# Four in-place split buffers for the weight slabs of a two-layer transformer block in fp32

## What is computed

```python
z = rmsnorm(x, ln1) @ w_in
merged = (sigmoid(ga) * (o_a @ w_pa) + sigmoid(gb) * (o_b @ w_pb)
          + sigmoid(gc) * (o_c @ w_pc))
x = x + merged @ w_o
u = causal_dwconv(rmsnorm(x, ln2) @ w_up, conv_w, conv_b)
a, b = split(u, 2)
x = rmsnorm(x + (silu(a) * b) @ w_down, ln_f)
# second layer
y = concatenate([y_conv, y_rwkv]) @ w_out          # both from rms_norm(x, g0) @ w_in_2
x = x + rms_norm(y, g1)
y = memory_cross_attention(rms_norm(x, g2), mem_n, wq, wkv, wo)
x = x + rms_norm(y, g3)
y = swiglu(rms_norm(x, g4), w_gu, w_down_2)
x = x + rms_norm(y, g5)
```

## Time and profile before

| what | us |
|---|---|
| median of three executions | 914.25 |
| the profiled execution | 913.55 |
| its span in the profile | 911.7 |
| PE busy in it | 858.5 (94%) |
| DVE busy | 567.5 (62%) |
| ACT busy | 440.0 (48%) |
| POOL busy | 20.8 (2%) |
| transfers | 145.86 MB, 160 GB/s in the mean |

### The profile page before, as it was taken

One profiled execution on the slowest core, in us unless ns is written; L12 is line 12 of the kernel. 1 busy time (PEld: TensorE's weight loads), 2 busy tenths in 40 slices (PEclk: granted clock), 3 DMA queues, 4 the chain that ended last, 5 costly groups with the idle time before them and its releaser, 6 DMA issues.

```text
span 911.7 us, 18606 instructions
## 1 busy us (share of the span) xinstructions
PE 858.5 (94%) x7952; PEld 797.7 (87%) x7952; DVE 567.5 (62%) x671; ACT 440.0 (48%) x558; POOL 20.8 (2%) x31
## 2 busy tenths in 40 slices
PE   4999999998999999998988989999899799999997
PEld 4899999987999998888986889888897799999885
DVE  4475467476777776647599886566554655555444
ACT  4555755445555556436472401445544544444333
POOL 1110000000000002000000000000000000000000
PEclk9999999999999999999999999999999799999999
DMA  9853433556455555455433121144524355555541
GB/s 346 287 183 115 173 139 139 186 208 220 160 176 180 184 179 191 179 185 202 168 125 110 48 96 50 48 155 160 171 95 141 112 185 184 184 184 184 185 139 46
DMA packets 22253, 145.86 MB, mean 160 GB/s; under 512 B 2618, under 2 KB 2810, under 8 KB 6064
## 3 DMA queue, kind: packets, MB, share of 16 engines
q1 hardware_dynamic: 19008, 134.23, 42.2%
q0 software_dynamic: 2896, 10.13, 3.4%
q10 hardware_dynamic: 288, 0.59, 0.2%
HBM read 143.87 MB, written 1.07 MB: 159 GB/s over the span
## 4 chain that ended last, share of the span: by engine, by line
PE 79%; DVE 12%; ACT 4%; issue 3%; DMA 1%; DVEq 0%; ACTq 0%
PE ps L1629 23%; PE ps L1631 22%; PE ps L1630 22%; DVE w_lo L935 4%; ACT w_hi L470 2%; PE ps L2025 2%; PE ps L1973 1%; PE ps L1657 1%; DVE cacc L1293 1%; DMA norm_gain<-in_rows_vec 1%; DVE xn L1525 1%; PE ps L2190 1%; PE ps L2206 1%; DVE xn L989 1%; DVE x L1531 1%
## 5 line engine op out<-in xcount | busy, mean ns | idle before, releaser
L935 DVE TENSOR_TENSOR w_lo<-raw,w_hi 128x2048 fp32r<-128x2048 f32 x124 | 284.8, 2297 | 189.2 <-ACT w_hi L470 189.2
L1629 PE MATMUL ps<-hT_hi,w_hi 128*128 128x256 f32 x1240 | 356.2, 287 | 13.2 <-DVE hT_lo L996 7.1
L1630 PE MATMUL ps<-hT_lo,w_hi 128*128 128x256 f32 x1240 | 352.9, 285 | 0.0
L1631 PE MATMUL ps<-hT_hi,w_lo 128*128 128x256 f32 x1240 | 352.9, 285 | 0.0
L470 ACT ACTIVATE w_hi<-raw 128x2048 fp32r<-128x2048 f32 x125 | 239.1, 1912 | 174.6 <-PE ps L1631 174.1
L1629 PEld LDWEIGHTS ps<-hT_hi,w_hi 128*128 128x128 f32 x1240 | 240.2, 194 | 19.0 <-issue 16.1
L1630 PEld LDWEIGHTS ps<-hT_lo,w_hi 128*128 128x128 f32 x1240 | 240.1, 194 | 0.1
L1631 PEld LDWEIGHTS ps<-hT_hi,w_lo 128*128 128x128 f32 x1240 | 240.1, 194 | 0.0
L1629 PE MATMUL ps<-w_hi,gT_hi 128*128 128x512 f32 x176 | 69.8, 397 | 0.6 <-DVE w_lo L935 0.6
L1631 PE MATMUL ps<-w_hi,gT_lo 128*128 128x512 f32 x176 | 69.0, 392 | 0.0
L1630 PE MATMUL ps<-w_lo,gT_hi 128*128 128x512 f32 x176 | 68.4, 388 | 0.0
(11 more groups left out here) (286 smaller groups left out, 1043.2 us busy)
## 6 DMA issues: line engine op xcount, KB each, us to landing
raw<-in_weights SPq DMA_DIRECT2D x126, 1024.0 KB, 4.9
row_gain<-in_rows_vec POOLq DMA_DIRECT2D x4, 512.0 KB, 4.8
norm_gain<-in_rows_vec POOLq DMA_DIRECT2D x4, 512.0 KB, 4.7
bias<-bias_scratch POOLq DMA_DIRECT2D x1, 1536.0 KB, 9.5
x<-in_x SPq DMA_DIRECT2D x2, 512.0 KB, 5.2
xn<-in_mem POOLq DMA_DIRECT2D x2, 512.0 KB, 5.8
out<-x SPq DMA_DIRECT2D x4, 256.0 KB, 2.1
masks<-in_masks POOLq DMA_DIRECT2D x1, 768.0 KB, 12.4
```

The costliest lines, as they stand in the source:

```text
L935: V.tensor_tensor(w_lo[:, n % SPLIT, :], raw[:, n % RAW, :], w_hi[:, n % SPLIT, :].bitcast(F32), ALU.subtract).then_inc(sems["lo_ready"], 1)
L1629: mm(dst, left[0], right[0], start=first, stop=False)
L1630: mm(dst, left[0], right[1], start=False, stop=False)
L1631: return mm(dst, left[1], right[0], start=False, stop=last)
```

## The change

`w_lo` gets the memory of `raw`: it is laid over it with four buffers, so DVE overwrites each loaded slab by its low half. `w_hi` gets four buffers too; the total memory stays the same. A load into a buffer may then start only when PE has used the slab before in it, so SP waits for `slab_used` in place of `lo_ready`, and ACT's own wait for `slab_used` is gone. All `splits` and the splits in the loops reach one slab further (`AHEAD = 1`). At five places a call of `splits` is moved behind `fill_normed` or shortened by one slab, and `split_around` gives way to a whole split after the gating.

```diff
 RAW = 4
-SPLIT = 2
+AHEAD = 1
...
-        raw = sb("raw", [P, RAW, SLAB])
-        w_hi = sb("w_hi", [P, SPLIT, SLAB], F32R)
-        w_lo = sb("w_lo", [P, SPLIT, SLAB], F32R)
+        whole = ExitStack()
+        raw = sb("raw", [P, RAW, SLAB], F32, whole)
+        whole.close()
+        w_lo = sb("w_lo", [P, RAW, SLAB], F32R)
+        w_hi = sb("w_hi", [P, RAW, SLAB], F32R)
...
# SP
-                    sp.wait_ge(sems["lo_ready"], turn * RAW + (s + 1))
+                    sp.wait_ge(sems["slab_used"], turn * RAW + (s + 1))
...
# ACT, split and splits
-                if n >= SPLIT:
-                    act.wait_ge(sems["slab_used"], n - SPLIT + 1 + SLABS_PER_TURN * turn)
-                A(w_hi[:, n % SPLIT, :], raw[:, n % RAW, :], ACT.Copy).then_inc(sems["hi_ready"], 1)
+                A(w_hi[:, n % RAW, :], raw[:, n % RAW, :], ACT.Copy).then_inc(sems["hi_ready"], 1)
-                while next_slab[0] <= min(last, SLABS - 1):
+                while next_slab[0] <= min(last + AHEAD, SLABS - 1):
...
# ACT and DVE, the loops
-                    split(n + s + 2, turn)
+                    split(n + s + 2 + AHEAD, turn)
...
# DVE
-            split_around(gate_place(8)[0], lambda: gated(1, 0))
-            for q in range(1, 4):
+            for q in range(4):
                 gated(1, q)
-                if q == 2:
+                if q == 0:
                     outputs(3)
+            splits(gate_place(8)[0])
...
-            splits(FIRST_SLAB["up"])
+            splits(FIRST_SLAB["up"] - 1)
             add_acc("w_o")
             normed("ln2")
             fill_normed("ln2")
+            splits(FIRST_SLAB["up"])
...
             normed("g0")
+            fill_normed("g0")
             splits(FIRST_SLAB["in2"])
-            fill_normed("g0")
...
             normed("g2")
+            fill_normed("g2")
             splits(FIRST_SLAB["wq"])
-            fill_normed("g2")
...
-            splits(FIRST_SLAB["gu2"])
             add_normed("y3", 2)
             normed("g4")
             fill_normed("g4")
+            splits(FIRST_SLAB["gu2"])
```

More of the change, by code:

```diff
@@ L380, in _ @@
             for n in range((turns + 1) * RAW, SLABS):
-                sp.wait_ge(sems["lo_ready"], n - RAW + 1)
+                sp.wait_ge(sems["slab_used"], n - RAW + 1)
                 sp.dma_start(raw[:, n % RAW, :], weights[n]).then_inc(raw_in[n % RAW], 16)
@@ L670, in _ @@
                 up_pair(2, turn)
-            next_slab[0] = FIRST_SLAB["down"] + 2
+            next_slab[0] = FIRST_SLAB["down"] + 2 + AHEAD
             g_high(0, PAIRS - 1)
@@ L898, in gu_pair @@
                 n, u = FIRST_SLAB["gu2"] + 2 * p, FIRST_UNIT["gu2"] + 2 * p
-                split(n + 1, turn)
+                split(n + 1 + AHEAD, turn)
                 src = unit(u, turn)
@@ L906, in gu_pair @@
                     gu_high(p - 1, turn)
-                split(n + 2, turn)
+                split(n + 2 + AHEAD, turn)
             def gu_high(p, turn=0):
@@ L918, in _ @@
                 gu_pair(2, turn)
-            next_slab[0] = FIRST_SLAB["down2"] + 1
+            next_slab[0] = FIRST_SLAB["down2"] + 1 + AHEAD
             gu_high(PAIRS - 1)
@@ L934, in split @@
                 dve.wait_ge(sems["hi_ready"], n + 1 + SLABS_PER_TURN * turn)
-                V.tensor_tensor(w_lo[:, n % SPLIT, :], raw[:, n % RAW, :], w_hi[:, n % SPLIT, :].bitcast(F32),
+                V.tensor_tensor(w_lo[:, n % RAW, :], raw[:, n % RAW, :], w_hi[:, n % RAW, :].bitcast(F32),
                                 ALU.subtract).then_inc(sems["lo_ready"], 1)
             def splits(last):
-                while next_slab[0] <= min(last, SLABS - 1):
+                while next_slab[0] <= min(last + AHEAD, SLABS - 1):
                     split(next_slab[0])
                     next_slab[0] += 1
-            def split_around(n, between):
-                dve.wait_ge(sems["hi_ready"], n + 1)
-                for half in range(2):
-                    cols = slice(half * SLAB // 2, (half + 1) * SLAB // 2)
-                    ins = V.tensor_tensor(w_lo[:, n % SPLIT, cols], raw[:, n % RAW, cols],
-                                          w_hi[:, n % SPLIT, cols].bitcast(F32), ALU.subtract)
-                    if half == 0:
-                        between()
-                ins.then_inc(sems["lo_ready"], 1)
-                next_slab[0] = n + 1
             def do(instruction):
@@ L1613, in slab @@
                 pe.wait_ge(sems["lo_ready"], n + 1 + SLABS_PER_TURN * turn)
-                return w_hi[:, n % SPLIT, :], w_lo[:, n % SPLIT, :]
+                return w_hi[:, n % RAW, :], w_lo[:, n % RAW, :]
             def used(instruction):
@@ L1673, in first_features @@
                 bank_free(u)
-                hi, lo = w_hi[:, n % SPLIT, :], w_lo[:, n % SPLIT, :]
+                hi, lo = w_hi[:, n % RAW, :], w_lo[:, n % RAW, :]
                 for c in range(2):
```

## The result

The changed kernel takes 908.5 us in the median of four executions (908.15 to 910.1), where the kernel before took 915.0 beside it (914.17 to 915.99). The ratio is 0.9932, with a 95% interval of 0.9915 to 0.9949: 6.5 us less, faster by more than 0.2%, as forecast, but about two thirds of the 9.5 us forecast, and the time, 908.51 us unrounded, lies just above the upper end of the range (901.5 to 908.5). Two later groups of executions of the same file gave 0.9931 [0.9904, 0.9958] and 0.9921 [0.9897, 0.9945], with single times from 904.5 to 911.5 us. The profiled execution took 908.15 us, its span is 906.4 (911.7 before).

What follows compares the result with a forecast made beforehand. PE was taken as the bound, busy 858.5 of 911.7 us, with short stalls from a one-slab lookahead. Terms 4.7 + 0 + 1.6 + 1.5 + 0.5 + 1.5 - 0.3 = 9.5 us gave 904.5 us, range 901.5 to 908.5.

Steps and rivals of the forecast that it cites:

- the price of moving the loads: Loads issued at a slab's use instead of its split: -0.3 us at the start, the one place where it costs.
- the clock at the convolution: Second layer's convolution: a longer gap might lower the clock, but small matmuls are paced by issue; 0 taken, bound -1.6 us.
- The waits for low halves: PE's eight waits for `w_lo`, 7.8 us: 4.7 us gained; the projection's 3.1 us return at the convolution, so 0 there.
- The fills: Activations' low halves ahead of the slab's split: 1.6 us gained at `in2` and 1.5 us at `wq`.
- The fourth rival: Saved waits come back elsewhere, as at the convolution, and only the fills count: 911.1 us; chance 0.04.
- The additions ahead of `gu2`: Ahead of `gu2`, the next slab's split is released sooner, so the serial chain starts sooner: 0.5 us gained, bounds 0 to 0.7.
- The start: The sixth slab lands late amid the bias gathers, delaying its split and PE's first transposes: -0.3 us, bounds 0 to -3.
- Rival 3: At the start, the sixth slab lands some 3 us later under two gathers; PE waits at the first transposes: 907.5 us; chance 0.1.
- a sign of being wrong: In steady stages, ACT idling for loads would mean landings beyond 5.5 us and the prediction wrong.
- the prediction's own account of the ring: Steady stages: a load lands 5.1 us after the use of m-4, its split starts at 5.5; low halves have 7 us of slack.
- The clock at `wq`: After `wq`, the gap cut to 1.9 us causes no fall of the clock: 1.5 us gained, bounds 0 and 1.6.
- rival 1: The clock gives nothing back, or the convolution gives back what `wq` gains: 906.0 us; chance 0.2.

Runs made afterwards that it cites:

- e3: The kernel before with only the reordered fills at `in2` and `wq` (activations' low halves ahead of the slab's split): 918.6 us, ratio 1.0038.
- e1: The changed kernel with the load of the seventh slab also held until both gathers of the attention bias have landed: 903.1 us, ratio 0.9883 to the kernel before.
- a2: The changed kernel executed again, unchanged, in a later group: 909.1 us, ratio 0.9921 to the kernel before.
- e4: e1 plus four matmuls of the identity that add nothing, issued while TensorE waits for `glu` ahead of the convolution: 903.3 us, ratio 0.9884 to the kernel before.
- e5: e1 with five convolution taps moved on VectorE from after the sixth slab of `in2` to after the seventh, behind `glu`: 903.4 us, ratio 0.9875.
- e6: e1 with the load of slab 79 also held until the recurrence's next products are done: 902.1 us, ratio 0.9861 to the kernel before.
- a1: The changed kernel executed again, unchanged, in a later group: 909.7 us, ratio 0.9931 to the kernel before.
- e7: e1 plus matmuls of the identity that add nothing while TensorE waits for normalised activations at ln2, `wq` and ahead of `gu2`: 901.1 us, ratio 0.9844.
- e9: The kernel before with only the release changed, loads issued when PE has used the slab four places earlier: 921.1 us, ratio 1.006.

## Why the prediction was right and wrong, point by point

The step that failed is the price of moving the loads. The prediction took it as 0.3 us at the start and nothing elsewhere; the runs showed 3 us at the start and 1.8 in the recurrence. A second term, the clock at the convolution, was taken at 0 and cost 1.5.

**The waits for low halves: right.** All eight went; the 3.1 us in the projection of the second layer came back at the convolution, whose wait rose by 3.34 (1.59 to 4.93), against a value of 4.7 forecast.

**The fills: right in size, wrong in what makes them.** The gap at `in2` fell from 1.61 us to 0.32 (1.6 forecast, 1.3 found), that at `wq` from 3.41 to 2.24, 1.2 for 1.5. The step took them for the worth of the reordering; e3 shows that alone it loses 3.5 us. The prediction had the slab ready ahead of time, which only the lookahead gives. The fourth rival ("only the fills count", 911.1) did not come: outside the projection the saved waits didn't come back elsewhere.

**The additions ahead of `gu2`: right.** 0.5 forecast, 5.82 to 5.25 found. The like wait ahead of `up`, of which nothing was counted, fell from 3.36 to 2.71, 0.65 us that the prediction missed.

**The start: the step that failed most.** -0.3 was taken, with bounds 0 to -3; it was -3.0 (2.07 + 0.91), and 3.3 by the edit of e1. The prediction followed the sixth slab into its split and forward to PE. That slab was early enough (it landed 5.1 us after its issue and was split at 36.6, not at 38.7). It never turned the question round: what does a load do to the transfer that it meets? The gathers were named as the cause of a slow load, and they were the victim: the second landed at 46.5 us instead of 42.3, DVE stood 4.68 us for it, and behind DVE stood ACT and PE. Rival 3 had the size (907.5, chance 0.1) and the symptom, PE waiting at the first transposes, by another chain. A further 0.69 us at 135.56 comes from what the text did foresee, ACT's evacuation queued behind a split that waits for its load (6.87 us there). ACT also idled for loads in steady stages, which the prediction listed as a sign of being wrong: 3.29 us at 395.73, in `down`. It cost nothing there, and landings were not late (4.9 us in the median); by the prediction's own account of the ring ACT had to wait for each landing, so that sign was badly chosen. The 4.4 us that the prediction sets beside these 4.9 are from the Trainium skill's fit ("DMA: Bandwidth & Descriptors", section "Anatomy of one DMA") for transfers that GpSimd issues, and the slabs' loads are SyncE's; no term rests on it. The "9 us before the first matmul's data exist" are 10.3 in the profile, which changes no term.

**The clock at `wq`: an expectation where a lottery was due.** 1.5 us were counted as gained in full. After the same 2.24 us the clock fell in five profiles (the first, a2, e4, e5, e6) and not in two (a1, e1). Without a fall the stretch from `wq` to `gu2` takes 70.6 us, with one 71.9 to 73.3. The term was worth less than half of 1.5 in the mean.

**The clock at the convolution: rival 1.** 0 was taken for the falling clock there, with the bound -1.6; the first profile lost 1.54 (13.21 to 14.75), the mean of seven profiles is 1.1.

**The recurrence: not seen.** -1.8 us, from a load that the new release moved to where PE takes a 16 KB packet of instructions about every 4 us. The prediction's sentence that loads come later and that only ACT feels it missed a second user of the DMA engines.

**A gain not seen.** Both profiles have PE's 7952 matmuls in one order, so they can be compared one by one. From the first matmul of `up` to the end of that stage the lead of the changed kernel grows from 1.3 to 2.4 us, by about 0.2 every four slabs, without a wait worth a row; another 0.9 comes in the same way from the start of the gates to `w_o`, and in `down` only 0.1. PE's timeline of the kernel before at the start of a slab, and of the changed kernel:

```profile
311.83 0.28 PE L1629 MATMUL ps<-hT_hi,w_hi 128*128 128x256 f32 x1
...
312.21 0.38 PE L1629 MATMUL ps<-hT_hi,w_hi 128*128 128x256 f32 x1
...
312.67 0.28 PE L1629 MATMUL ps<-hT_hi,w_hi 128*128 128x256 f32 x1
```

```profile
311.72 0.28 PE L1618 MATMUL ps<-hT_hi,w_hi 128*128 128x256 f32 x1
...
312.08 0.28 PE L1618 MATMUL ps<-hT_hi,w_hi 128*128 128x256 f32 x1
...
312.44 0.28 PE L1618 MATMUL ps<-hT_hi,w_hi 128*128 128x256 f32 x1
```

The step from one k to the next is 0.36 us; at the start of a slab it was 0.38 and 0.46 and is now 0.36. A twentieth of a microsecond a slab in the mean, over the 22 slabs of `up`, is hidden from the table of waits. That a slab ready just before its use costs this is read from the rows; no run varied the slack alone.

**The sum.** 4.7 + 1.3 + 1.2 + 0.6 + 0.65 gained (low halves, fills, additions), less 3.0 (start) + 0.7 (at 135.56) + 0.2 (the wait for `glu` beyond the 3.1) + 1.5 (clock at the convolution) + 1.8 (recurrence), is 1.25 of the 5.3 us by which the spans differ. Matmul by matmul, 2.1 to 2.2 more is the gain not seen; 0.5 came in the first 20 us; and 0.5 is the clock at ln2, which fell in the kernel before (4.45 us from the wait for xn to `up`) and not in this execution (3.93; a1 and a2 have 4.45 and 4.39). The rest, some 0.9, is mostly steps of about 0.15 beside each wait that went. The mechanism held; three terms of cost, 6.3 us together at the start, the convolution and the recurrence, were taken at 0.3. That the time came out only 4 us above the forecast is partly luck: gains in no term of the sum made up for more than half of what was lost.

## What to carry to other kernels

When a change moves transfers in time, list not only who waits for them but whom they now meet: other transfers with a deadline, and the engine's own instruction fetch; holding back one load gave 3.3 us here, and another 2. Reordering work and looking further ahead can be one edit: the order pays only when the work passed over is already done, so price such parts together or by turns. A wait of 2 to 5 us on TensorE costs itself plus, more often than not, about 1.5 us of lower clock behind it, and matmuls that add nothing, issued into the wait, kept the clock up here. They gave 3.6 us ahead of ordinary groups (e7), and nothing that the times could tell ahead of the convolution (e4), whose small matmuls lose less by the lower clock.

## What the runs showed of the hardware that was not expected

- A 768 KB gather took 12.2 us beside a 1.5 MB gather and one whole 1 MB load (e1), and 15.5 and 15.8 us beside two such loads (the changed kernel, e9).
- TensorE can stop for 1.5 to 2.1 us among small matmuls while a 1 MB load runs or has just run, with nothing waited for; in the recurrence it did so in eight of nine profiles with the load and in none of five without. A 16 KB packet of the queue "instruction" then came 6.2 to 6.5 us after the one before instead of 3.4 to 4.3, and PE resumed 1.4 to 1.6 us after its end.
- After a wait of 2.24 us the granted clock fell in five of seven profiles of kernels that are the same there.
- A subtraction that writes over its own input took 2302 ns, and 2297 ns when it wrote elsewhere.
